# Output weights of the expert pairs sent from ScalarE's queue instead of SyncE's

## What is computed

```
h2 = rmsnorm(x, norm2_w)
logits = h2 @ router_w + router_b            # 32 experts, top 4 of each token, softmax weights
for each expert e, over its tokens xb:
    gu = xb @ w_gate_up[e] + b_gate_up[e]    # 1024 x 2048
    gate = min(gu[:, 0::2], 7);  up = clip(gu[:, 1::2], -7, 7)
    y  = ((up + 1) * gate * sigmoid(1.702 * gate)) @ w_down[e] + b_down[e]   # 1024 x 1024
    out[tokens] += y * weight
x = rmsnorm(x + out, final_norm_w)
```

## Time and profile before

| what | us |
|---|---|
| median of 3 runs | 1121.64 (1120.76 to 1122.49) |
| the profiled execution, its own time | 1122.86 |
| its span, from first to last instruction | 1121.0 |
| PE busy | 1080.7 (96%) |
| ACT busy | 223.1 (20%) |
| bytes moved | 438.85 MB, 391 GB/s over the span |

### The profile page before, as it was taken

One profiled execution on the slowest core, in us unless ns is written; L12 is line 12 of the kernel. 1 busy time (PEld: TensorE's weight loads), 2 busy tenths in 40 slices (PEclk: granted clock), 3 DMA queues, 4 the chain that ended last, 5 costly groups with the idle time before them and its releaser, 6 DMA issues.

```text
span 1121.0 us, 14756 instructions
## 1 busy us (share of the span) xinstructions
PE 1080.7 (96%) x6261; PEld 529.3 (47%) x6261; DVE 347.5 (31%) x685; ACT 223.1 (20%) x355; POOL 47.9 (4%) x38
## 2 busy tenths in 40 slices
PE   7999999999999999999999999998999999999996
PEld 7889888734343434343443434333343434343432
DVE  4894888422222130312222221110303030302222
ACT  6645774301010101010101010101010101010002
POOL 0392000000000000000000000000000000000000
PEclk9999999999999999999999999999999999999999
DMA  9547549999999999999999999999999999999995
GB/s 317 198 152 305 221 159 391 379 398 416 416 432 431 429 433 433 434 431 433 430 433 433 431 431 430 430 430 430 432 431 433 433 431 431 430 431 431 427 427 238
DMA packets 35486, 438.85 MB, mean 391 GB/s; under 512 B 2884, under 2 KB 5720, under 8 KB 20472
## 3 DMA queue, kind: packets, MB, share of 16 engines
q1 hardware_dynamic: 34528, 437.76, 92.9%
q10 hardware_dynamic: 920, 0.56, 0.2%
HBM read 437.25 MB, written 1.05 MB: 391 GB/s over the span
## 4 chain that ended last, share of the span: by engine, by line
PE 75%; DMA 13%; DVE 2%; another core or an unknown queue 1%; issue 1%; SPq 1%; ACT 0%; DVEq 0%
PE PS L1808 33%; PE PS L1869 17%; DMA W<-in_w_down_dram 8%; DMA W<-in_w_gate_up_dram 4%; PE PS L1758 4%; PE PS L1778 4%; PE PS L1852 3%; PE PS L1462 2%; PE PS L1466 2%; PE PS L1469 2%; PE PS L1828 2%; PE PS L1448 1%; PE PS L1889 1%; DVE w_lo L463 1%
## 5 line engine op out<-in xcount | busy, mean ns | idle before, releaser
L1808 PE MATMUL PS<-W,M 128*64 128x512 f32 x2048 | 456.3, 597 | 17.4 <-DMA W<-in_w_gate_up_dram 12.2
L1808 PEld LDWEIGHTS PS<-W,M 128*64 128x64 f32 x2048 | 142.6, 137 | 300.7 <-issue 279.1
L1869 PE MATMUL PS<-W,M 128*64 128x512 f32 x1024 | 226.8, 594 | 9.2 <-DMA W<-in_w_down_dram 9.1
L1281 DVE TENSOR_SCALAR M<-PS 128x256 f32<-128x256 f32 x64 | 27.0, 422 | 512.0 <-PE PS L1808 512.0
L1869 PEld LDWEIGHTS PS<-W,M 128*64 128x64 f32 x1024 | 73.7, 137 | 147.8 <-issue 141.5
L861 ACT ACTIVATE M<-M 128x256 f32<-128x256 f32 x64 | 26.7, 417 | 473.9 <-DVE M L1281 473.9
L866 ACT COPY M<-PS 64x512 f32<-64x512 f32 x31 | 17.9, 578 | 268.4 <-PE PS L1869 268.4
L1297 DVE COPY M<-PS 128x512 f32<-128x512 f32 x32 | 22.1, 692 | 130.8 <-PE PS L1852 130.8
L1758 PE MATMUL PS<-M,X 128*128 128x128 f32 x480 | 57.6, 278 | 0.0
L1778 PE MATMUL PS<-M,SELT 128*128 128x512 f32 x120 | 55.8, 606 | 0.0
L1758 PEld LDWEIGHTS PS<-M,X 128*128 128x128 f32 x480 | 54.7, 192 | 1.0
(11 more groups left out here) (267 smaller groups left out, 856.0 us busy)
## 6 DMA issues: line engine op xcount, KB each, us to landing
W<-in_w_gate_up_dram SPq DMA_DIRECT2D x52, 4096.0 KB, 42.8
W<-in_w_down_dram SPq DMA_DIRECT2D x26, 4096.0 KB, 45.1
W<-in_w_gate_up_dram SPq DMA_DIRECT2D x23, 2048.0 KB, 12.3
raw<-in_w_in_dram SPq DMA_DIRECT2D x10, 2048.0 KB, 8.5
W<-in_w_down_dram SPq DMA_DIRECT2D x9, 2048.0 KB, 12.3
W<-in_w_down_dram SPq DMA_DIRECT2D x5, 1024.0 KB, 45.2
raw<-in_w_out_dram SPq DMA_DIRECT2D x2, 2048.0 KB, 10.5
raw<-in_w_in_dram SPq DMA_DIRECT2D x2, 1024.0 KB, 9.1
```

The lines of the kernel that those rows point to most:

```text
L1281: v.tensor_scalar(gate[b], g2[:, :, 0], LIMIT, None, ALU.min).then_inc(gate_ready, 1)
L1808: ins = mm(gu[half][64 * g:64 * g + 64, :], hTe[:, k, tok], gu_slot[slot][:, kk, c:c + 512], start=(k == 0), stop=(k == KD - 1))
L1869: ins = mm(dst[64 * n:64 * n + 64, :], actT[b][:, 4 * kh + k, :], dn_slot[slot][:, k, 512 * n:512 * n + 512], start=(kh == 0 and k == 0), ...
```

## The change

From pair 0 to pair 13, ACT sends the output weights of the next pair, so those of pairs 1 to 14: unit 8/9 behind the copy of A's product (`drain_y(p * 2, 0)`), unit 10/11 behind the copy of B's product. SP stops after unit 6/7 in the pairs 1 to 14 (`stop=8`); it still sends all of pair 15. The output weights of pair 1, which went slot by slot, now go as two units (`by_slots`), and PE no longer waits for slots 9 and 11 apart in that pair. ACT's loop over the pairs becomes straight code, since the transfer's source address differs from pair to pair.

```
         def by_slots(j, m, first_round):

-            return not first_round or j < 2 or j == PAIRS - 1
+            return not first_round or j == 0 or j == PAIRS - 1 or (j == 1 and m < 8)
...
             for j in range(1, last):
-                load_pair(j, 2 * j, j, True)
+                load_pair(j, 2 * j, j, True, stop=8)
...
-            def pair(p, last=False):
+            def load_output_weights(p, b):
+
+                m = 8 + 2 * b
+                se.dma_start(slots(m, 2), unit_src(2 * p + 2, m)).then_inc(slot_loaded[m], 16)
+
+            def pair(p, last=False, loads=False):
                 expert(p * 2, 0)
                 se.wait_ge(selT_filled, p + 1)
                 nc.scalar.copy(selT, gath[:, 0:T]).then_inc(selT_drained, 1)
                 expert(p * 2 + 1, 1)
                 drain_y(p * 2, 0)
+                if loads:
+                    load_output_weights(p, 0)
                 if last:
                     se.wait_ge(y_filled, p * 2 + 2)
                     nc.scalar.copy(Y[64:128, 0:512], gu[0][0:64, :]).then_inc(y_ready, 1)
                 else:
                     drain_y(p * 2 + 1, 1)
+                    if loads:
+                        load_output_weights(p, 1)

             se.wait_ge(rounds_ready, 1)
             most = se.value_load(CMI[0:1, 0:1], min_val=0, max_val=T)
-            with se.Fori(0, E // 2 - 1) as p:
-                pair(p)
+            for p in range(PAIRS - 1):
+                pair(p, loads=p < PAIRS - 2)
             pair(E // 2 - 1, last=True)
```

## The result

The changed kernel takes 1141.33 us, the median of five runs (1136.69 to 1142.67); the kernel before, timed with it, 1121.64 us (1120.14 to 1124.18). The ratio is 1.0174, with a 95% interval of 1.0156 to 1.0192: by the ratio 19.5 us slower (the medians lie 19.7 us apart), where 18 us were predicted (1139.6 us). Another four runs of the changed kernel, on another chip, gave 1.0172 (1.0155 to 1.0189).

The account below looks back on a forecast made before the run. Weight transfers were taken as the bound. Later issue 3.6, landing order 12.3 or 17.3 and clock 1.5 us summed to 17.4 or 22.4; 18 was taken, giving 1139.6 us, range 1124.5 to 1147.

Parts of the forecast that it names:

- What bounds the kernel: Weight transfers bound throughout: a pair's six units take 58.4 us at 431 GB/s, PE's own work 53.3 us.
- Issue cost and cover: ACT's 28 added issues of 0.33 us and straight code cost nothing, covered by 268.4 us of ACT idle time.
- Later issue in pair 1: At the stage's start, pair 1's output units go out behind ACT's copies and the second lands later: +3.6 us.
- Order of landing: Output weights land ahead of sooner-needed unit 6/7, leaving PE more work: +12.3 us (last wait in pair 13) or +17.3 (14).
- The walk through the pairs: Pairs 4 to 13 at half rate per queue: PE waits for unit 6/7 about every second pair, long ones 8 to 10 us.
- The clock: After the last long wait PE runs at its lower clock level of 1.2 GHz for a while: +1.5 us.
- The sum: Start, order and clock add to 17.4 us with the last wait in pair 13, 22.4 in pair 14; 18 taken.
- How the queues share: SP's and ACT's queues each get half of the DMA engines while both hold work; chance 0.70.
- Arrival order: Rival: both queues served in order of arrival, units land as before but for pair 1: +3.6, 1125 us; chance 0.14.
- SP first: Rival: SP's queue served ahead of ACT's, PE waits for output weights: +37 to +80, 1160 to 1205 us; chance 0.08.
- Not slower: Rival: two queues close small holes between transfers, 434 GB/s against 431, giving 1119.5 us; chance 0.05.
- What would show it: Waits of 7 to 10 us for gate and up weights, DMA full until about 1113 us, PE's last 12 to 20 wait-free.

Follow-up runs that it names:

- pairs 12 and 14 alone: Two runs: the changed kernel, but ACT sends only pair 12's or only pair 14's output weights; 1.0062 and 1.0149 against the kernel before.
- the straight code: The changed kernel with ACT's loop written out, but SP sending all weights in order; 0.9998 against the kernel before.
- pairs 1 to 8: The changed kernel, but ACT sends the output weights of pairs 1 to 8 only, SP those of 9 to 15; 1.0011 against the kernel before.
- both transfers late: The changed kernel, but ACT sends both output units behind the second product, unit 8/9 12 us later; 1.0234 against the kernel before.
- One queue with the same disorder: SP sends all weights, but in pair 14 unit 6/7 goes last, behind 8/9 and 10/11; 1.0152 against the kernel before.
- the second profile: Another profiled execution of the unaltered changed kernel, with a more usual time than the first; span 1140.0 us.

## Why the prediction came out right, step by step

- **What bounds the kernel.** Right. The rate stayed at 431 to 432 GB/s, and PE's own 53.3 us a pair held: it wins back 4.9 us a pair by pairs 12 and 14 alone, for the 5.1 said.
- **Issue cost and cover: nothing.** Right: 28 issues from ACT and the straight code make no difference that shows (0.9998 for the code, 1.2 us in all with the 16 issues of pairs 1 to 8).
- **Later issue in pair 1: +3.6 us.** Wrong in size: about 1 us. Two things in it failed. The issue isn't held until both copies of the product are through. ACT's timeline in the changed kernel, at pair 0's first product:

```profile
264.47 0.58 ACT L866 COPY M<-PS 64x512 f32<-64x512 f32 x1 [4.92 <-PE PS L1878]
264.48 0.35 ACTq L872 DMA_DIRECT2D W<-in_w_down_dram  x1
265.06 0.58 ACT L867 COPY M<-PS 64x512 f32<-64x512 f32 x1
```

  The transfer goes out 0.01 us after the first copy starts, not 1.2 us behind. And the whole hole was taken as a delay. The hole is there: 380 and 352 GB/s against 431 and 403 before are 1.2 MB or 2.8 us of transfers, and the first of the 16 engines to end its part of pair 2's first unit ends it 2.9 us later. But a landing is the slowest engine's, and that one ends only some 1 us later: the 16 engines end this unit 2.2 us apart before and 0.3 us apart after. That a pause lets the slowest engine catch up fits this; why an engine falls behind, no run shows. With both transfers late the hole was 13.7 us of transfers and 9 us did come out at the end, so this cover has an end.
- **Order of landing: +12.3 or +17.3 us.** Right, and in both forms: 12.4 us (15.0 - 2.6) in the profile where the last long wait is in pair 13, with the short wait in pair 14 in it, and 16.3 (19.2 - 2.9) where it is in pair 14. The work left was a little misread, and the errors nearly cancel: 26.7 us from slot 6 to the end of a late pair for the 26.3 of pair 1, and 49.7 for pair 15 (1074.70 to 1124.35) for 50.5, which held small waits of before. One queue with the same disorder gives 17.1 us in all. I took pair 13 for the likelier; the median is that of pair 14, to judge by its time.
- **The walk through the pairs.** Right in kind, with waits for unit 6/7 at every second pair, and too long in size: 5.9 us where 8 to 10 were said, as the short waits between them (0.7 to 1.1 us) were missed, and as in the second profile pairs 12 to 14 wait 3.2 each. The need for unit 6/7 was put 80 us into a pair; at 58.4 us a pair, by which 8/9's 92 is counted, it is 85. The sum doesn't hang on the length of a wait, only on the work left when the last one ends.
- **The clock: +1.5 us.** Too small: 2.6 us in one profile, 2.9 in the other, at 0.50 each time. The 1.5 us were read behind one wait of 3.27 us; behind the last long waits for weights 16 matmuls took 6.24 and 6.59 us for 3.65. The price varies: 1.4 us (5.04 for 3.65) behind a wait of 3.22 in the second profile.
- **The sum.** 18 predicted, 19.5 measured. The start was some 2.6 us too dear, the clock 1.1 to 1.4 us too cheap, and the last wait lay in the dearer pair in most runs, to judge by their times (some 4 us by the traces). For that pair the sum was 22.4 us. So the mechanism was right, and part of the closeness of 18 to 19.5 is luck: the errors offset one another.
- **How the queues share: about half each.** Right: 23.4 to 24.7 us for a unit that alone needs 9.73. ACT's one small transfer that landed next to SP's was no sign of arrival order. The turns are of one row, and not of whole transfers as that row seemed to say.
- **Rivals.** Arrival order would have left PE's waits at 2.5 us and the landings of ACT's queue at 40 us or more: 24.7. SP first would have shown waits for output weights: none. Not slower would have needed more rate: 432 against 430 GB/s, and the time lost elsewhere. For SP first, 37 to 80 us on 1121.6 are 1159 to 1202, not 1160 to 1205.
- **What would show it.** The DMA engines were empty from 1108 us, not 1113, as the start cost only some 1 us. PE works on from there without a wait for 16 us, up to 1124.4, and in the second profile for 20; 12 to 20 were said.

The Trainium skill's page "DMA: Bandwidth & Descriptors" (section "Rules for kernel authors") says that spreading transfers over issuing engines brings no bandwidth. The trace agrees, with 432 and 431 GB/s against 430 and 431; what it cost here is the order.

## What to carry to other kernels

When a stream of transfers is the bound and its consumer takes them as they land, a second queue that carries part of it changes the order of landing, and each unit that lands too early delays one that is needed sooner by as much as it takes itself (8.6 us for one, 18.7 for two of 9.73). This shows as waits of an engine while the DMA engines are full, and it costs only what the consumer can't win back before the end: the same two transfers cost 16.7 us in pair 14, 6.9 in pair 12, and those of pairs 1 to 8 all together 1.2. So read from the last long wait on: the work left behind it against the transfers left behind it.

## What the runs showed of the hardware

- Two queues of SP and ACT share the DMA engines row by row: 23.6 us for 4096 KB with rows of 32 KB on both, 18.6 with 16 KB rows on the other queue, about 32.5 with 16 KB rows on its own.
- ACT sent a transfer 0.01 us after the start of the copy that is written ahead of it in its program, and didn't wait for its end. A place behind a copy in the program doesn't hold a transfer until the copy is done.
- The 16 engines ended the same transfer 2.2 us apart in one trace and 0.3 us in another. A missing 1.2 MB (2.8 us) against before put the first engine 2.9 us later and the landing 1 us; a missing 5.9 MB (13.7 us) cost 9.
- After waits of 3.4 and 5.9 us the granted clock was 0.50, the lower level of 1.2 GHz, and the 16 matmuls behind them took 6.59 and 6.24 us for 3.65: 2.9 and 2.6 us.
- The same program showed two patterns of late waits, 0.7, 5.9 and 0.9 us or 3.1, 3.2 and 3.4 us in pairs 12 to 14, with spans of 1134.8 and 1140.0 us. What chooses between them no run here tells.
